# The experts' scatter adds its rows onto x in DRAM, and x is read back

## The reference

```python
def hmoe(x, w_rg, b_rg, w_re, b_re, w_g, w_u, w_d):
    ...
    wts = jax.nn.softmax(top_v, axis=-1) * g_p[:, None]
    eid = g_idx[:, None] * EXPERTS_PER_GROUP + top_i.astype(jnp.int32)
    ...
    def expert_block(args):
        xblk, e = args
        hid = jax.nn.silu(xblk @ w_g[e]) * (xblk @ w_u[e])
        return hid @ w_d[e]
    yb = lax.map(expert_block, (xb, blk_e)).reshape(p_len, d)
    y = jax.ops.segment_sum(yb * row_w[:, None], row_tok, num_segments=n + 1)
    return y[:n]

def run_trunk(x, cond, p, rope, ctx_k, ctx_v):
    for i in range(DEPTH):
        ...
        x = x + g1 * m
        h = rmsnorm(x, p['g_norm2'][i]) * (1 + sc2) + sh2
        y = hmoe(h.reshape(b * t, d), ...)
        x = x + g2 * y.reshape(b, t, d)
    return rmsnorm(x, p['g_final']), new_k, new_v
```

## Time and profile before

| | us |
|---|---|
| median of three runs | 1820.08 |
| lowest and highest run | 1818.83, 1826.5 |
| the profiled execution | 1818.77 |
| its span, from the first to the last instruction | 1816.6 |
| PE busy in it | 1555.7 (86%) |
| DVE, ACT, POOL busy | 616.1, 249.8, 247.0 |
| layer 0: row table, from its first product to the first block | 478.94 to 492.27 |
| layer 0: experts, from the first block to the last scatter's issue | 492.27 to 976.13 |
| layer 0: read-back issued to layer 1's first product | 979.75 to 1003.71 |
| layer 1: read-back issued to the end | 1788.11 to 1816.6 |

### The profile page before, as it was taken

The page is one execution under the profiler, slowest core; times in us unless marked ns, Lnnn a source line. Parts: engine busy times, 40 slices in busy tenths (PEclk is TensorE's granted clock), DMA queues, the critical chain, the costliest instruction groups (busy, mean ns, idle before and its releaser), DMA issues.

```text
span 1816.6 us, 19397 instructions
## 1 busy us (share of the span) xinstructions
PE 1555.7 (86%) x6764; PEld 725.7 (40%) x6764; DVE 616.1 (34%) x1194; ACT 249.8 (14%) x497; POOL 247.0 (14%) x376
## 2 busy tenths in 40 slices
PE   4999896689899988889894799999898989898982
PEld 2445444545533333333332344545433333333330
DVE  2499546723622212212113220323521212211224
ACT  2111034521100000000002111011000000000001
POOL 0024020000112111211110001000112121111110
PEclk9999999979899999999997899999899999999996
DMA  9753423031599999999995653253699999999984
GB/s 349 264 186 140 145 87 151 24 151 57 193 404 419 420 419 420 421 420 419 420 417 230 239 190 136 93 231 129 255 420 419 419 420 418 420 420 420 419 366 191
DMA packets 115566, 534.12 MB, mean 294 GB/s; under 512 B 15581, under 2 KB 16406, under 8 KB 65066
## 3 DMA queue, kind: packets, MB, share of 16 engines
q1 hardware_dynamic: 92944, 493.45, 67.4%
q0 software_dynamic: 12032, 21.08, 3.1%
q10 hardware_dynamic: 10522, 18.64, 2.9%
HBM read 522.55 MB, written 27.33 MB: 303 GB/s over the span
## 4 chain that ended last, share of the span: by engine, by line
PE 53%; DMA 17%; DVE 4%; issue 3%; ACT 2%; SPq 1%; ACTq 0%; POOLq 0%; DVEq 0%
PE psum_pair_B L1756 22%; DMA scratch<-w_up 15%; PE psum_pair_C L1774 10%; PE psum_pair_C L1696 4%; PE psum_pair_B L1656 4%; PE psum_pair_D L1696 4%; PE psum_pair_A L1656 3%; PE psum_pair_D L1763 1%; DVE scratch L1341 1%; ACT scratch L874 1%; DMA weight_ring<-w_ada 1%; PE psum_pair_C L1597 1%; PE psum_pair_C L1670 1%; SPq L489 1%; PE psum_pair_D L1689 1%
## 5 line engine op out<-in xcount | busy, mean ns | idle before, releaser
L1756 PE MATMUL psum_pair_B<-weight_ring,gates_by_token 128*64 128x512 f32 x1408 | 316.1, 601 | 31.4 <-DMA weight_ring<-w_up 21.4
L1756 PE MATMUL psum_pair_B<-scratch,gates_by_token 128*64 128x512 f32 x896 | 204.5, 609 | 18.4 <-DMA scratch<-w_up 18.4
L1341 DVE TENSOR_TENSOR scratch<-psum_pair_B,scratch 128x256 f32<-128x256 f32 x72 | 30.6, 425 | 533.6 <-ACT scratch L874 533.6
L1756 PEld LDWEIGHTS psum_pair_B<-weight_ring,gates_by_token 128*64 128x64 f32 x1408 | 117.3, 138 | 223.7 <-issue 223.7
L1774 PE MATMUL psum_pair_C<-weight_ring,scratch 128*64 128x512 f32 x704 | 160.8, 597 | 25.0 <-issue 22.5
L682 POOL DMA_INDIRECT expert_rows<-scratch,scatter_rows x72 | 73.4, 1020 | 740.8 <-DVE scratch L1353 740.8
L1656 PE MATMUL psum_pair_A<-scratch,weight_ring 128*128 128x128 f32 (+1 forms) x512 | 143.7, 439 | 4.4 <-DVE scratch L1392 2.8
L874 ACT ACTIVATE scratch<-psum_pair_B 128x256 f32<-128x256 f32 x72 | 27.7, 384 | 863.9 <-PE psum_pair_B L1756 863.9
L1656 PE MATMUL psum_pair_B<-scratch,weight_ring 128*128 128x128 f32 (+1 forms) x512 | 142.2, 436 | 0.0
L1756 PEld LDWEIGHTS psum_pair_B<-scratch,gates_by_token 128*64 128x64 f32 x896 | 77.5, 141 | 141.4 <-issue 141.4
L1435 DVE SCALAR_TENSOR_TENSOR weight_ring<-weight_ring,params 128x655 f32<-128x655 f32 x120 | 116.9, 974 | 5.0 <-DVE gates_by_token L1083 1.0
(11 more groups left out here) (359 smaller groups left out, 1478.2 us busy)
## 6 DMA issues: line engine op xcount, KB each, us to landing
weight_ring<-w_gate SPq DMA_DIRECT2D x44, 2048.0 KB, 29.0
weight_ring<-w_up SPq DMA_DIRECT2D x44, 2048.0 KB, 33.2
weight_ring<-w_down SPq DMA_DIRECT2D x44, 2048.0 KB, 33.8
weight_ring<-w_ada SPq DMA_DIRECT2D x24, 2048.0 KB, 8.8
scratch<-w_up SPq DMA_DIRECT2D x20, 2048.0 KB, 28.1
scratch<-w_down SPq DMA_DIRECT2D x20, 2048.0 KB, 28.0
scratch<-w_gate SPq DMA_DIRECT2D x20, 2048.0 KB, 22.4
weight_ring<-w_in_e SPq DMA_DIRECT2D x5, 2048.0 KB, 11.2
```

The source lines that it names most:

```text
L1341: tt(HID[par], PB[B_][:, 512 * par + 256:512 * par + 512], SIL[par], ALU.mult).then_inc(sig("hidden", l), 1)
L1756: ins = mm(PB[B_][CAP * q:CAP * (q + 1), 512 * par:512 * par + 512].rearrange("p (u n) -> p u n", u=2), XGT[par][:, at:at + CAP], w[:, :, ...
```

## The change

The tail stores each tile of x to DRAM (`kept`, on ACT's queue) as `summed_rows`, which has one place per token. The scatter adds its rows to what is there (`compute_op=ALU.add`), with the same row numbers as the gather, so the second table holds only the weights. A token's two rows may lie in consecutive blocks, so a scatter now waits for the one before it, by a single semaphore, and POOL's first scatter waits for x to be stored. At the layer's end SP reads the sum back into `X`, 512 KB per tile; DVE's additions are gone, and the scaling of layer 1's first norm goes from ACT to DVE. In each layer `keep_busy(4)` ahead of the row table becomes `keep_busy(8)`.

```diff
-        y_dram = nc.dram_tensor("expert_rows", [4 * TOK, D // 2], f32, kind="Internal").ap()
+        y_dram = nc.dram_tensor("summed_rows", [2 * TOK, D // 2], f32, kind="Internal").ap()
+        y_tiles = y_dram.rearrange("(t p two) d -> t p (two d)", p=128, two=2)
...
-            def expert_rows(l, t):
-                sp.dma_start(YB[t], rows[t]).then_inc(sig("tile_in", t), 16)
+            def summed_rows(l, t):
+                sp.dma_start(X[:, t, :], y_tiles[t]).then_inc(sig("tile_in", t), 16)
...
-                total = [sp.value_load(NSC[0:1, par:par + 1], min_val=16 * PAIRS, max_val=16 * PAIRS + 8 * OVER) for par in range(2)]
-                for par in range(2):
-                    sp.wait_ge(sig("scattered", l, par), total[par])
+                total = sp.value_load(NSC[0:1, 0:1], min_val=16 * NSTAT, max_val=16 * (NSTAT + OVER))
+                sp.wait_ge(sig("scattered", l), total)
...
-                    pool.wait_ge(sig("combined", 0), NT)
+                    pool.wait_ge(sig("tile_in", NT - 1), 32)
...
-                pool.wait_ge(sig("block_of_pair"), 2 * (l + 1))
-                pool.tensor_tensor(VAL[:, 1], EQ, rows_flat[1].unsqueeze(2).broadcast_to([128, 10, NBLK]), ALU.mult).then_inc(sig("row_values"), 1)
...
                 def scatter(b, par, before):
                     if before is not None:
-                        pool.wait_ge(scattered[par], before)
+                        pool.wait_ge(scattered, before)
...
-                    pool.tensor_copy(SI[par][:, :], IDX[:, bass.ds(b + NBLK, 1)]).then_inc(sig("scatter_rows_set", l), 1)
+                    pool.tensor_copy(SI[par][:, :], IDX[:, bass.ds(b, 1)]).then_inc(sig("scatter_rows_set", l), 1)
...
-                                            bounds_check=4 * TOK - 1, oob_is_err=False).then_inc(scattered[par], 16)
+                                            bounds_check=2 * TOK - 1, oob_is_err=False, compute_op=ALU.add).then_inc(scattered, 16)
...
-                pool.wait_ge(sig("routed"), l + 1)
+                pool.wait_ge(sig("x_stored"), 16 * NT * (l + 1))
                 scatter(0, 0, None)
                 gather(3, 1, 2)
-                scatter(1, 1, None)
+                scatter(1, 1, 16)
...
-                        scatter(b, par, 16 * it)
+                        scatter(b, par, 32 * it + 16 * par)
...
-                def scaled(t):
-                    act.wait_ge(sig("inverse"), t + 1)
-                    act.activation(XN[:, t, :], X[:, t, :], ACT.Copy, scale=rstd[:, t:t + 1]).then_inc(sig("normed", 1), 1)
...
-                    act.wait_ge(sig("combined", 0), t + 1)
+                    act.wait_ge(sig("tile_in", t), 32)
                     norm_tile(t, XN[:, t, :])
...
+                def kept(t):
+                    act.dma_start(y_tiles[t], X[:, t, :]).then_inc(sig("x_stored"), 16)
...
                     turned(t)
+                    if t:
+                        kept(t - 1)
...
                 stored(NT - 1)
+                kept(NT - 1)
...
-                act.wait_ge(sig("combined", 1), t + 1)
+                act.wait_ge(sig("tile_in", t), 48)
...
-                dve.wait_ge(sig("row_values"), l + 1)
-                tt(VAL[:, 2], EQ, small[:, 90:100].unsqueeze(2).broadcast_to([128, 10, NBLK]), ALU.mult).then_inc(sig("row_weights"), 1)
+                dve.wait_ge(sig("weights_known"), l + 1)
+                tt(VAL[:, 1], EQ, small[:, 90:100].unsqueeze(2).broadcast_to([128, 10, NBLK]), ALU.mult).then_inc(sig("row_weights"), 1)
...
-                        body(2 * it + par, par, 16 * it)
+                        body(2 * it + par, par, 32 * it + 16 * (par - 1))
...
-            def combine(l, t, halves=(0, 1)):
-                if 0 in halves:
-                    dve.wait_ge(sig("tile_in", t), 16 * (l + 2))
-                    link(tt(X[:, t, :], X[:, t, :], YB[t][:, 0:D], ALU.add))
-                if 1 in halves:
-                    tt(X[:, t, :], X[:, t, :], YB[t][:, D:], ALU.add).then_inc(sig("combined", l), 1)
...
+            def scaled(t):
+                inverse_root(t)
+                ts(XN[:, t, :], X[:, t, :], rstd[:, t:t + 1], None, ALU.mult).then_inc(sig("normed", 1), 1)
 
             def combined_norm():
 
                 for t in range(4):
-                    combine(0, t)
-                    if t:
-                        inverse(t - 1)
-                combine(0, 4, (0,))
-                inverse(3)
+                    scaled(t)
...
-            for t in range(NT):
-                combine(1, t)
...
-                keep_busy(4)
+                keep_busy(8)
...
-                    ins = mm(p[:, 768:768 + 2 * NBLK].rearrange("p (s b) -> p s b", s=2), POSH[:, i, :], VAL[:, 1:3, i, :], start=(i == 0), stop=(i == 9))
+                    ins = mm(p[:, 768:768 + NBLK], POSH[:, i, :], VAL[:, 1, i, :], start=(i == 0), stop=(i == 9))
```

More of the change, by code:

```diff
@@ L67, in shape_constants @@
                             np.arange(NBLK), np.arange(OVER), np.array(SEQ_OF), np.array([t - i for i, t in enumerate(TWICE_AT)])]).astype(np.float32)
-    rows = np.zeros((128, 2, 2, NT), np.float32)
+    rows = np.zeros((128, 2, NT), np.float32)
     tok = np.arange(NT)[None] * 128 + np.arange(128)[:, None]
-    for k in range(2):
-        rows[:, 0, k] = 2 * tok - NOROW
-        rows[:, 1, k] = 2 * (2 * tok + k) - NOROW
+    rows[:, :] = (2 * tok - NOROW)[:, None]
     half = NOROW + (np.arange(128, dtype=np.float32)[:, None] >= CAP)
@@ L230, in build @@
         BLKN = scr(RT + 25 + NT * 36, 10)
-        YB = [scr(2 * D * i, 2 * D) for i in range(NT)]
         GF = SQ[:, 516:516 + D]
@@ L452, in _ @@
             sp.dma_start(X[:, 4, :], a["x_prompt"][0]).then_inc(sig("tile_in", 4), 16)
-            rows = y_dram.rearrange("(t p four) d -> t p (four d)", p=128, four=4)
-            def expert_rows(l, t):
-                sp.dma_start(YB[t], rows[t]).then_inc(sig("tile_in", t), 16)
+            def summed_rows(l, t):
+                sp.dma_start(X[:, t, :], y_tiles[t]).then_inc(sig("tile_in", t), 16)
             for l in range(2):
@@ L662, in _ @@
                 gathered = [sig("gathered", l, i) for i in range(2)]
-                scattered = [sig("scattered", l, i) for i in range(2)]
+                scattered = sig("scattered", l)
                 def gather(b, par, turns):
@@ L711, in _ @@
                                 gather(i + (NSTAT + 2), par, i + (NSTAT + 1))
-                            scatter(i + NSTAT, par, 16 * it + 16 * PAIRS)
+                            scatter(i + NSTAT, par, 32 * it + 16 * (NSTAT + par))
         @block.scalar
@@ L1316, in routing @@
                 link(dve.tensor_copy(NBK[:, 1:1 + OVER], ebk))
-                later = tmp(OVER, where="near")
-                link(ts(later, iota["o"], ove[:, NE - 1:NE], None, ALU.is_lt))
-                link(dve.tensor_reduce(gs[:, 0:2], later.rearrange("p (i two) -> p two i", two=2), AX_X, ALU.add))
-                ts(NSC[:, :], gs[:, 0:2], 16.0, 16.0 * PAIRS, ALU.mult, ALU.add).then_inc(sig("scatters_counted"), 1)
+                ts(NSC[:, :], ove[:, NE - 1:NE], 16.0, 16.0 * NSTAT, ALU.mult, ALU.add).then_inc(sig("scatters_counted"), 1)
                 assert at["near"] <= SCR_N
@@ L1325, in slot_table @@
                 p = take(dve, "weights", l)
-                ts(IDX[:, NBLK:], p[:, 768:768 + NBLK], HALFROW, None, ALU.add)
                 w = SLOTW.rearrange("p (b c) -> p c b", c=2)
-                ts(w[:, 0], p[:, 768 + NBLK:768 + 2 * NBLK], 0.0, None, ALU.max)
-                took(ts(w[:, 1], p[:, 768 + NBLK:768 + 2 * NBLK], -1.0, 0.0, ALU.mult, ALU.max), "weights", l)
+                ts(w[:, 0], p[:, 768:768 + NBLK], 0.0, None, ALU.max)
+                took(ts(w[:, 1], p[:, 768:768 + NBLK], -1.0, 0.0, ALU.mult, ALU.max), "weights", l)
                 after(dve, "weights", l)
-                dve.memset(small[:, 106:107], 0.0).then_inc(sig("routed"), 1)
                 if l == 0:
@@ L1351, in body @@
                     if before is not None:
-                        dve.wait_ge(scattered[par], before)
+                        dve.wait_ge(scattered, before)
                     tt(YR[par], bank(C_, par), GS[par], ALU.mult).then_inc(sig("y_ready", l), 1)
```

45 lines of the change are left out of this document (17 added, 28 removed).

## The result

The changed kernel takes 1826.9 us (median of 20 runs), the kernel before 1820.7 us (median of 20 runs beside them). The ratio is 1.0037, 95% interval 1.0024 to 1.0051: 4 to 9 us slower. The ratio lies inside the 0.5% that was called "within", and the upper end of its interval just touches it. In a second measurement of the unaltered kernel it was 1.0030, 1.0012 to 1.0048.

The account below looks back on a forecast made before the run. The prediction took DMA traffic to bound the expert stage, other chains between stages. Terms: -8.6 - 5.0 - 9.7 + 1.0 + 26.5 = +4.2 us on 1818.8, forecast 1823 us; range 1803 to 1856, the forecast's own 1817 to 1829.

Parts of the forecast that it names:

- What bounds it: Expert stage: lasts as long as its DMA traffic, so added traffic lengthens it one for one.
- The scatter: Expert stage: reading the destination costs one more pass, 0.39 us for each of 68 scatters, 26.5 us lost in both layers.
- bounds that lay nine passes apart: Scatter's cost: 0 if the second read is hidden, at worst 3.55 us each, the price of nine passes more.
- Rivals 1 and 2: Scatter: second read hidden, 1796 us, chance 0.20; or an adding row costs several passes, 1876 us with three, chance 0.23.
- rival 4: Expert stage: scatters landing only after 15 us delay POOL 1.3 us at each block, giving 1911 us; chance 0.04.
- The landing: End of each layer: the last scatter lands later for its added read, 0.5 us each, 1.0 us lost.
- The ends of the layers: Halved read-back, no DVE additions, scaling off ACT: 5.0 us gained at layer 0's end, 9.7 at layer 1's.
- the 1.4 taken back for the transposes' clock: End of layer 0: PE's low clock slows transposes after the wait, cutting a 6.4 us gain to 5.0.
- The table: Row table before block 0: PE keeps its clock and POOL's multiplication goes, 4.3 us earlier in layer 0, 8.6 us gained altogether.
- Rival 3: Row table: the clock falls during the table product all the same, giving 1832 us; chance 0.08.
- The lower bound of the term, 0: Row table: if the clock falls all the same, nothing is left of the 8.6 us gain.
- What was costed at nothing: Stores of x, POOL's and the scatters' new waits, smaller second table, one count fewer, SP's single register load: 0 us.

Follow-up runs that it names:

- the add alone: The changed kernel, but layer 1's scatter writes without adding while layer 0's still adds; 1815.0 us, ratio 0.9982 to the kernel before.

## Why the prediction was right, point by point

**What bounds it: right.** The expert stage is DMA time, nearly one for one. A pass less shortened it by as much (the add alone, 12.6 us), a plain pass more lengthened it by a little more (15.2 and 14.1).

**The scatter: right, mechanism and size.** Forecast one further pass, 0.39 us for each of 68, 26.5 us; measured 13.2 + 12.7 = 25.9, or 0.38 each, and 26.3 in the mean over all profiled executions that do and don't add. The choice among bounds that lay nine passes apart was made by the nearest row, the queue's share of two like passes, and that row held. The Trainium skill's ratio for a reducing transfer in a ring of cores ("Collectives: The Full Stack", "The bandwidth ceiling: the fold count and why AG ≠ RS ≠ AR") had given an estimate of 24.6; the trace agrees with it nearly as well as with the forecast, since the scatters' part of the queue went from 2.85 (half of 5.7) to 5.95%, a factor of 2.1 against the page's 1.93. Rivals 1 and 2 fall, and rival 4 with them. Its sign, waits of the scatter for the one before, did appear, 70 of them; it was badly chosen, since these waits take the place of waits for DVE. None was above 7.8 us, and the chain without the add costs nothing.

**The landing: near enough.** 0.0 and 0.6 us in the two profiles, and 0.7 in either layer in the mean over all, for a forecast of 0.5 each.

**The ends of the layers: right mechanism, undersized.** 6.6 for 5.0 and 10.5 for 9.7 in the two profiles. At the first the profile of before was a short one: 23.96 us from read-back to product, where the four other kernels with that code took 26.1 to 26.7, and the seven with the changed code took 16.4 to 18.9. In the mean the gain is 8.3 us, so the 1.4 taken back for the transposes' clock, for which no row gave the size, had better been left out, and 2 us more lay there. At the second the chain was hit closely: 14.88 us from read-back to last store for 15.7; the gain is 10.7 in the mean.

**The table: the term that was mis-sized.** "PE lost its clock after 5.5 us of idleness; I expect it to keep it over 2 us" was read from one fall in each layer, at 5.51 us, and no row showed what 2 us do. At 2.08 us the clock was kept in two stages of ten with this table and lost in eight; at 0.37 us it was kept in four of four. Rival 3 was this case, and got 0.08; its mechanism (small products alone after the idle time) is the one that the traces show, its price, 8.6 us back, holds for an execution that loses the clock in both layers. The lower bound of the term, 0, was also too high: with the fall the narrow second table makes the stretch 0.2 to 1.6 us longer than before. In the mean the ten stages took 13.0 us, and the four with the table and the four products of before 13.1 (13.33, 13.42, and 12.58 and 13.14 in the kernel that scatters twice). So in place of 8.6 us the term gave some 0.2, an estimate from these fourteen stages.

**So the number was near in part by luck.** The forecast of 1823.0 lies 3.9 us below the median of 1826.9. Of that 1.9 is the starting point, the profiled execution of 1818.8 where the median before is 1820.7, and 2.0 the difference, +6.2 measured (4.4 to 9.3 by the interval) for +4.2. From the means over all profiled executions the difference is 26.3 + 1.4 - 8.3 - 10.7 - 0.2 = +8.5: some 8 us too much gain for the table were offset by some 4 too little for the ends, and +8.5 is within the measured interval. With ten products, where the table's 7.1 us are there in every profile, the same sum is 8.7 - 7.1 = +1.6, and the kernel measures 1.0001, which is -3 to +4 us.

**What was costed at nothing:** the stores of x left no trace (the distance between the two profiles is the same ahead of the first of them and behind the last, and from the rank products that count the rows to the table product it is 9.7 us, before and changed), the chain neither; the narrow table is the exception.

## What to carry to other kernels

In a stage that DMA engines fill, as here, an adding scatter is to be costed as two passes over its bytes, even though the profile's bytes don't show the second; it pays only where the additions that it saves lie on a path longer than that, and here 17 to 19 us of shorter layer ends didn't pay for 26. An idle time of TensorE ahead of a run of small products should be closed fully, not halved: a clock that one profile shows as kept can be lost in the next, so such a gain is to be looked at in several executions. And the two parts of a change that have nothing to do with the add (the unread products, ten of them, and POOL's multiplication out of DVE's way) are worth more alone, 0.37%, than together with it.

## What the runs showed of the hardware beyond what was expected

- An adding scatter costs POOL more time as well: 1.60 us an instruction against 1.02, and the gap holds inside one execution (0.98 to 1.65 on the one line that did both).
- Its packets are more numerous for the same bytes: POOL's queue had 7538 in layer 0's stage, 5440 before. Half as long rows (7563 packets, 7.26 MB) took 61% of the scatters' engine time, not 50%, if the gathers are put at half of the plain queue's 5.5%.
- The granted clock can fall after TensorE has begun to work again: after 2.08 us of idleness it went from 1.00 to 0.50 between 1.4 and 3.0 us into a run of small products, in 13 of 16 profiled stages. After 0.37 us of idleness it didn't in four stages.
- POOL's multiplication beside DVE's one-hot product lengthens DVE's from 0.44 to 1.37 us; behind it, DVE's takes 0.44 us.
